# Reordering the first steps of three mixtures of experts: tile sums, router logits, and one step of the shared expert

## The reference

```python
def second_block(x, ...):
    for i in range(DEPTH_2):
        h = rmsnorm(x, norm_w[i, 0]) * (1.0 + sc1) + sh1
        y = short_conv_mixer(...) if i % 2 == 0 else gated_deltanet_mixer(...)
        x = x + gt1 * rmsnorm(y, norm_w[i, 1])
        h = rmsnorm(x, norm_w[i, 2]) * (1.0 + sc2) + sh2
        y = hier_moe(h, ...)
        x = x + gt2 * rmsnorm(y, norm_w[i, 3])

def hier_moe(h, ...):                  # 64 experts in 8 groups, two per token
    gl = xt @ w_rg + b_rg              # group logits
    el = xt @ w_re + b_re              # expert logits
    ...                                # best group, two best experts in it, gates
    out = (silu(xb @ w_gate[e]) * (xb @ w_up[e])) @ w_down[e]   # per expert
    y = scatter_add(out * gate)
    ys = (silu(xt @ ws_gate) * (xt @ ws_up)) @ ws_down          # shared expert, width 512
    y = y + sigmoid(xt @ w_sg) * ys
```

## Time and profile before

| | us |
|---|---|
| median of 3 runs | 2630.17 (2624.46 to 2630.81) |
| the profiled execution | 2629.6 |
| its span | 2627.8 |
| PE busy in the span | 2165.7 (82%) |
| DVE busy | 1246.3 (47%) |
| ACT busy | 775.6 (30%) |
| POOL busy | 209.4 (8%) |

### The profile page before, as it was taken

The page is one execution under the profiler, slowest core; times in us unless marked ns, Lnnn a source line. Parts: engine busy times, 40 slices in busy tenths (PEclk is TensorE's granted clock), DMA queues, the critical chain, the costliest instruction groups (busy, mean ns, idle before and its releaser), DMA issues. The chain is left out here.

```text
span 2627.8 us, 43428 instructions
## 1 busy us (share of the span) xinstructions
PE 2165.7 (82%) x18238; PEld 1520.7 (58%) x18238; DVE 1246.3 (47%) x1974; ACT 775.6 (30%) x1303; POOL 209.4 (8%) x204
## 2 busy tenths in 40 slices
PE   5999999896974899887778766899998897768766
PEld 3977777794542789543334335677777643334433
DVE  3367676644323444543333335666555643334334
ACT  4266666431112423311111114444423411111112
POOL 2000000101101000000000002111111000000001
PEclk8999999896997899899889887999999999989988
DMA  9157675428997322899999982211113699999995
GB/s 354 45 192 245 221 242 187 127 97 336 385 421 291 108 96 113 337 397 417 419 419 415 415 355 82 65 50 50 43 49 137 243 366 416 419 418 414 412 416 210
DMA packets 211851, 684.69 MB, mean 261 GB/s; under 512 B 23022, under 2 KB 122039, under 8 KB 152503
## 3 DMA queue, kind: packets, MB, share of 16 engines
q1 hardware_dynamic: 198742, 646.01, 64.0%
q0 software_dynamic: 8912, 21.04, 2.3%
q10 hardware_dynamic: 3984, 14.68, 1.4%
HBM read 671.68 MB, written 21.00 MB: 264 GB/s over the span
## 5 line engine op out<-in xcount | busy, mean ns | idle before, releaser
L221 PE MATMUL PS<-second 128*128 128x256 f32 (+1 forms) x4944 | 931.0, 346 | 54.0 <-DVE second L251 21.8
L221 PEld LDWEIGHTS PS<-second 128*128 128x128 f32 x4944 | 760.9, 193 | 200.6 <-DVE second L251 29.1
L221 PE MATMUL PS<-ring,arena 128*32 128x256 f32 (+5 forms) x6288 | 667.6, 456 | 212.5 <-DMA ring<-in_moe_w_down 67.0
L221 PEld LDWEIGHTS PS<-ring,arena 128*32 128x32 f32 (+2 forms) x6288 | 316.9, 125 | 450.0 <-issue 309.4
L221 PE MATMUL PS<-arena 128*32 128x256 f32 (+10 forms) x2480 | 499.6, 383 | 77.0 <-DMA ring<-in_moe_w_up 22.2
L221 PEld LDWEIGHTS PS<-arena 128*32 128x32 f32 (+4 forms) x2480 | 248.2, 151 | 242.4 <-issue 172.8
L233 ACT ACTIVATE arena<-PS 128x512 f32<-128x512 f32 (+1 forms) x217 | 106.1, 489 | 589.4 <-PE PS L221 504.5
L240 DVE TENSOR_TENSOR arena<-PS,arena 128x512 f32<-128x512 f32 (+1 forms) x305 | 210.6, 690 | 100.4 <-PE PS L221 73.5
L240 DVE TENSOR_TENSOR arena<-arena,PS 128x256 f32<-128x256 f32 (+1 forms) x77 | 41.0, 532 | 411.0 <-PE PS L221 409.9
L233 ACT ACTIVATE arena<-arena 128x128 f32<-128x128 f32 (+4 forms) x299 | 176.1, 589 | 201.4 <-DVE arena L240 69.6
L240 DVE TENSOR_TENSOR second<-ring,second 128x1024 fp32r<-128x1024 f32 (+1 forms) x90 | 149.0, 1656 | 157.5 <-ACT second L233 151.7
(11 more groups left out here) (166 smaller groups left out, 1380.8 us busy)
## 6 DMA issues: line engine op xcount, KB each, us to landing
ring<-in_moe_w_down SPq DMA_DIRECT2D x124, 1024.0 KB, 16.3
ring<-in_moe_w_up SPq DMA_DIRECT2D x121, 1024.0 KB, 15.4
ring<-in_moe_w_gate SPq DMA_DIRECT2D x109, 1024.0 KB, 16.5
ring<-in_ada_w SPq DMA_DIRECT2D x48, 1024.0 KB, 5.4
arena<-in_moe_w_gate SPq DMA_DIRECT2D x28, 1024.0 KB, 11.7
ring<-in_w_mod SPq DMA_DIRECT2D x22, 1024.0 KB, 7.0
arena<-in_moe_w_up SPq DMA_DIRECT2D x19, 1024.0 KB, 14.8
spare<-in_moe_w_gate SPq DMA_DIRECT2D x17, 1024.0 KB, 15.7
```

Of the source, the lines that this page charges most:

```text
L221: return P.e.matmul(o, l, r, start=st, stop=sp)
```

## The change

Three edits. First, in `add_rows_ve` the normalisation of tile 2 moves behind tile 3's sums and its addition to x, and in `add_rows_ac` tile 3's `rsqrt` moves ahead of `h2T_ac` of tile 0 (mixtures 1 and 2). Second, in `moe_pe` the transposes of tile 2 and 3 come before the logits of tile 1 and 2 (all mixtures). Third, one step of the shared expert instead of two stands between the list of tokens and the first turn, and `SIDE[0]` grows from 1 to 2, so that step 4 follows `gate_up_pe` of unit 0 (mixtures 1 and 2).

```diff
@@ add_rows_ve
-            if t:
+            if t in (1, 2):
                 norm_mixed_ve(name, t - 1)
...
             stt(x[:, t, :], XN[:, t, :], rs[:, t:t + 1], x[:, t, :], ALU.mult, ALU.add, "x", name, t)
+        norm_mixed_ve(name, 2)
         h2T_ve(m, 1)
@@ add_rows_ac
+            A.wait_ge(at("ssq", name, t))
+            rsqrt(rs[:, t:t + 1], F, "sq", name, t)
             if t == 3:
                 h2T_ac(m, 0)
-            A.wait_ge(at("ssq", name, t))
-            rsqrt(rs[:, t:t + 1], F, "sq", name, t)
             again_ac(name, t)
@@
-    SIDE = (1, 2, 1, 2, 2, 1, 2, 1, 0, 2, 2, 2, 2)
+    SIDE = (2, 2, 1, 2, 2, 1, 2, 1, 0, 2, 2, 2, 2)
@@ moe_pe
-            if t:
-                logits_pe(m, t - 1)
+            if t == 1:
+                logits_pe(m, 0)
+        for t in (1, 2):
+            logits_pe(m, t)
         logits_pe(m, 3).then_inc(*P.mark("ps", "L", m.i))
...
         tokens_pe(m, "tok", 0, m.NS)
-        for _ in range(2):
-            next(more, None)
+        next(more, None)
@@ moe_ve, moe_ac
-            for _ in range(4):
+            for _ in range(3):
                 next(more)
...
-            for _ in range(4 * (n == 0) + side_steps(n)):
+            for _ in range(3 * (n == 0) + side_steps(n)):
```

## The result

The changed kernel takes 2646.28 us, the median of six runs (2645.6 to 2648.6), against 2629.94 for the kernel before beside it (six runs, 2624.46 to 2630.81). The ratio is 1.0067, with an interval of 1.0056 to 1.0077: 16.3 us slower, where 12.4 were forecast. The profiled execution took 2648.6 us, its span is 2646.9. PE was busy 2170.4 us (2165.7 before).

The account below looks back on a forecast made before the run. Mixtures 1 and 2 were taken as bound by their DMA loads. Losses of 8.4 + 4 = 12.4 us on the profiled 2629.6 give 2642.0; with the median 0.6 higher, 2642.5 us was predicted, 8 in 10 within 2631 to 2651.

Parts of the forecast that it names:

- The gate of SP's list: Mixtures 1 and 2: the load of shared-expert piece 3 waits for step 4, holding 8.5 MB issued behind it.
- Rival 3: Step 4 does not gate piece 3; buffers free earlier, mixtures end 4.9 us earlier: 2625 us, chance 0.07.
- How late piece 3 is: Step 4 ends later, so piece 3 and all behind it on SP are issued 11.9 us later in both mixtures.
- the clock: Mixture 1, gate and up of unit 0: if PE's granted clock falls, 1.7 us more; forecast would be 2644.2.
- The head start h: First two edits: last logits, routing, token list and gather come 0.4 us earlier in mixture 1, 2.0 in mixture 2.
- PE's lateness at turn 1: Step moved against earlier start: PE reaches turn 1 later by 1.9 us in mixture 1, 0.2 in mixture 2.
- rival 1: Loads far enough ahead, outage refilled, only PE's order counts: 2.1 us, 2632 us, chance 0.17.
- What is paid back: Late loads fill former DMA gaps: 3.5 us in mixture 1, leaving 8.4; 8.7 in mixture 2, leaving 3.2, taken as 4.
- Rival 2: Nothing repaid, late loads still wait for PE marks: 23.8 us over both mixtures, 2654 us, chance 0.14.
- The signs: Among others: unit 1's down matmuls wait over 8 us in mixture 1; turn 0 waits about 2 us for its gather.

Follow-up runs that it names:

- e1: Kernel before with the third edit alone (step 4 of the shared expert behind gate and up of unit 0): 2645.66 us, ratio 1.0059.
- e4: Kernel before, with only SP made to wait at piece 3 until gate and up of unit 0 are done: 2641.82 us, ratio 1.0047.
- e7: Changed kernel with step 4 between gate and up of unit 0 instead of behind both: 2641.80 us, ratio 1.0036.
- e8: Kernel before, unchanged, run again for a second profile: 2634.65 us.
- e2: Kernel before with the first two edits alone, both shared steps still ahead of turn 0: 2628.12 us, ratio 0.9990.
- e6: Kernel before with the first two edits; SP waits for unit 0's gathered rows after piece 2, piece 3 behind unit 0's down matrices: 2626.18 us, ratio 0.9979.
- e5: Changed kernel with piece 3 behind unit 0's down matrices and SP waiting after piece 2 for unit 0's gathered rows: 2640.32 us, ratio 1.0031.
- e3: Changed kernel with SP issuing piece 3 behind unit 0's down matrices, without waiting for the gather: 2652.87 us, ratio 1.0074.
- e9: Kernel before with SP issuing piece 3 behind unit 0's down matrices, without waiting for the gather: 2633.10 us, ratio 1.0020.

## Why the prediction was right, point by point

**The gate of SP's list: right.** e1, e4 and e7 move piece 3 in three different ways and each loses time; the DMA share is 0.00 in the window before it goes. Rival 3 wanted it issued by 1089 and 2093, which is about 37 us from the first load; it went at 50.5 and 51.3.

**How late piece 3 is: 14.0 and 14.2 us, not 11.9.** The difference comes from three terms, all in the rows (against the first profile of before; against the second, turn 0 of mixture 1 starts 4.7 us earlier and piece 3 goes 11.6 later):

| us | mixture 1, forecast | measured | mixture 2, forecast | measured |
|---|---|---|---|---|
| turn 0 starts earlier | 1.6 | 2.3 | 3.3 | 1.7 |
| turn 0 to step 4 | 10.15 | 12.73 | 11.84 | 12.41 |
| step 4 | 3.5 | 3.7 | 3.5 | 3.7 |

In mixture 1 it is the clock. The granted clock was 0.50, the lower level of 1.2 GHz, in the window at 1083, behind PE's wait for the gather (2.76 us) and its wait for DVE that stands in both kernels (2.07 us). From the first matmul of gate and up to the next step it took 9.57 us (1082.74 to 1092.31) instead of 7.04 (1091.12 to 1098.16). I had named this as 1.7 us, left it out of the sum and kept it in the range. The rule of the Trainium skill (TensorE: Matmul & The Clock Gate, "Part 1: The HAM clock gate") spoke for it, and the trace agrees: the lower clock stands right behind the idle time. It is not shown to be the edit's doing: e8 has such a fall (0.68) in the kernel before, without any wait for the gather.

The head start h was off in both mixtures. In mixture 1 the last logits ended 1.7 us earlier from the first load (14.4 against 16.1, and 18.5 in e8) where 0.4 was forecast; in mixture 2 it was 0.6 (16.1 against 16.7) where 2.0 was, and turn 0 gained 1.7, not 3.3. The same two edits gave 2.9 us there in e2 and e6. In e2 the granted clock was 1.00 in that stretch (2066 to 2075); in the changed kernel it was 0.50 from 2072 to 2077, while PE transposed.

The sum also moved the gather without changing its length. It was issued 1.7 us earlier in mixture 1 and took about 5.1 us, until PE's wait for it ended; in mixture 2 of e6, issued 2.9 us earlier than before, it took 6.6. An earlier gather meets more of the begin's own loads.

**PE's lateness at turn 1: put too small.** The forecast was 1.9 and 0.2 us; it is 5.3 and 4.0 (57.0 against 51.7, 57.9 against 53.9 from the first load; e8 has 55.8 and 53.9). The table's terms explain most of it, and the rest is a wait I had not seen. Step 5 now follows step 4 at once, and stands 1.36 us for ACT, which must first empty the bank. Before, the whole of gate and up of unit 0 lay between them. In e7, where step 4 stands apart from step 5, that wait is gone. I had written that PE is "hardly late", and gave that no price beyond rival 1's. It has one, but how much is not settled: with the list freed and PE as late, e5 loses 8.9 us in all, yet only 0.9 in mixture 2.

**What is paid back: right in kind, and too much in mixture 2.** Of 14.0 us of outage mixture 1 shows 11.0 (or 6.0 of 11.6, against the second profile), and of 14.2 mixture 2 shows 8.0, where 8.4 and 4 were forecast. So mixture 2 got 6.2 back and not 8. The sum was low by 3.9 us, and mixture 2's term alone was low by 4.0: 2.3 for the longer outage and 1.7 for what it did not get back. That these two agree is in part luck, since mixture 1's term may be off by 2.6 or by 2.4 the other way, and the stages that were put at nothing moved too. Rival 2, nothing repaid, would have been 2654, and the gaps filled at 1112 and 2120 speak against it. Rival 1, nothing but PE's order, would have been 2632; e4, with PE's order of before, costs 10.6 us.

**The signs.** The down matmuls of unit 1 wait 5.01 us in mixture 1, not over 8, because PE reaches them late too: they start at 106.9 us from the first load, against 98.8 and 104.9 in the two profiles of before. In mixture 2 they wait 6.46 us. Turn 0's wait for its gather, forecast at about 2 us, is 2.76 and 2.20.

**What stays open.** The stage between the mixtures, where PE is the bound, is 476 us in the four kernels with all three edits (after, e3, e5, e7) and 470 to 474 in all others. No instruction was moved there. The rows put the difference on PE: as many matmuls (4633 and 4637 records) are busy 424.0 us before (1600 to 2055) and 430.7 after (1604 to 2066), with the granted clock 0.94, 1.00 and 0.96 in its three windows before and 0.93, 0.99 and 0.93 after. Why it was granted less is open, and nothing was tried that would tell chance from cause. The 16.3 us may hold 3 to 6 of it. The whole loss is not the clock's: two runs of e4 took 2638.9 and 2639.4 us at a mean granted clock of 0.926 and 0.927, and the runs of the kernel before beside them at 0.925 to 0.928 took 2627.0 to 2633.7. How mixture 1's 11.0 or 6.0 is to be shared between the edit and its own variation of 5 us also can't be settled from one profile each.

## What to carry to other kernels

When loads are issued from one list in order, each wait in it is a gate for all behind it. Before moving work on the engine that frees a buffer, find which load waits for that buffer and how many megabytes stand behind it; here one step of 3.5 us, moved back, held 8.5 MB for up to 14 us in each of two mixtures, and the change cost 16. Freeing the list is no repair by itself: what it releases can run into the one small transfer that the next step waits for.

## What the runs showed of the hardware

A gather of 128 rows of 4 KB took 4.3 and 4.4 us when the loads ahead of it were ending (in mixture 1 before, the DMA share fell from 0.92 to 0.48 around it), and 9.2 and 8.0 us when two 1 MB loads had been issued up to 1.3 us before it by SP (e3, e9). In e6, with no such load but more of the begin's loads still in flight, it took 5.2 and 6.6 (in mixture 2 the DMA share over the 4.4 us behind its issue was 1.02, against 0.71 in the kernel before). It was issued by another engine, but met them. The Trainium skill (DMA: Bandwidth & Descriptors, "Issuing engines are not separate DMA queues") says that transfers of all issuing engines run on the same 16 DMA engines and interleave; the trace agrees. And one and the same program took 5 us longer over mixture 1 in a second execution, and over mixture 2 the same to 0.1 us.
